# One encoder layer on one core: convolution tiles made four ahead, query tiles transposed inside the last output product, first weight loaded in parts

## The reference, cut to what matters

```python
def token_mixer(x, ...):             # x: 1024 prompt rows and 8 x 16 sample rows of 1024
    proj = x @ w_in                  # query and latent parts, gates gb, gc, gv
    ...                              # attention of 8 heads (prompt: chunk-causal; sample: 512 cached rows too)
    u = gc * gv
    conv = cw[0]*u[s-2] + cw[1]*u[s-1] + cw[2]*u[s]
    return concat(attn, gb * conv) @ w_out
mk, mv = mem @ w_xk, mem @ w_xv      # 256 memory rows
x1 = LN1(alpha*x + token_mixer(x))
x2 = LN2(alpha*x1 + softmax((x1 @ w_xq) mk^T * scale) mv @ w_xo)
x3 = LN3(alpha*x2 + moe(x2))         # 32 gated experts, two per row
```

## Time and profile before

| what | us |
|---|---|
| median of 3 runs (1803.07 to 1812.1) | 1804.54 |
| the profiled execution, its own time | 1816.85 |
| its span, first to last instruction | 1815.0 |
| TensorE busy | 1653.2 (91% of the span) |
| VectorE busy | 1011.5 (56%) |
| ScalarE busy | 756.0 (42%) |
| GpSimd busy | 236.3 (13%) |

### The profile page before, as it was taken

How to read it: one execution, slowest core, us unless ns; L and a number is a source line. 1 busy time by engine, 2 the same in 40 slices (tenths; PEclk the granted TensorE clock), 3 DMA queues, 4 the chain that set the end, 5 groups by cost and what they waited for, 6 DMA issues and landing times.

```text
span 1815.0 us, 21425 instructions
## 1 busy us (share of the span) xinstructions
PE 1653.2 (91%) x8118; PEld 1280.6 (71%) x8118; DVE 1011.5 (56%) x1365; ACT 756.0 (42%) x1077; POOL 236.3 (13%) x192
## 2 busy tenths in 40 slices
PE   6999999799998797999989999699999999999965
PEld 3466666477667575899977777678888888888852
DVE  0301111166664375512244444698889889988946
ACT  0211221233335200222241212188777778788844
POOL 0000000000003165000011110111111111111104
PEclk9899999999999899999999987699999999999998
DMA  9401111420001443410034444489999999999967
GB/s 383 144 9 64 62 56 44 163 77 18 19 12 47 162 140 116 149 49 24 12 116 151 148 143 151 169 326 378 367 369 385 382 393 382 383 385 384 370 249 301
DMA packets 134692, 348.59 MB, mean 192 GB/s; under 512 B 24514, under 2 KB 27074, under 8 KB 129364
## 3 DMA queue, kind: packets, MB, share of 16 engines
q1 hardware_dynamic: 125396, 328.60, 49.2%
q0 software_dynamic: 9216, 18.89, 2.7%
HBM read 320.09 MB, written 42.10 MB: 200 GB/s over the span
## 4 chain that ended last, share of the span: by engine, by line
PE 60%; DMA 17%; DVE 13%; ACT 4%; issue 3%; SPq 2%; POOL 1%; DVEq 0%; POOLq 0%; ACTq 0%
DMA beside<-in_w_exp_up 13%; PE M L1118 9%; DVE rounded L1568 8%; PE M L683 8%; PE M L877 8%; PE T L723 6%; PE M L782 3%; PE T L674 3%; PE T L772 3%; PE M L674 2%; PE T L929 2%; PE T L930 2%; PE T L931 2%; PE M L956 2%; PE M L943 2%
## 5 line engine op out<-in xcount | busy, mean ns | idle before, releaser
L1118 PE MATMUL M<-rounded 128*128 128x512 f32 x2304 | 548.9, 395 | 13.4 <-DVE conv_w_rows L1883 7.7
L1118 PEld LDWEIGHTS M<-rounded 128*128 128x128 f32 x2304 | 430.0, 189 | 106.8 <-issue 16.0
L1568 DVE TENSOR_TENSOR rounded<-beside,rounded 128x1024 fp32r<-128x1024 f32 x395 | 462.8, 1217 | 63.1 <-ACT rounded L1454 55.3
L1454 ACT CAST rounded<-beside 128x1024 fp32r<-128x1024 f32 x256 | 260.3, 1049 | 96.1 <-DMA beside<-in_w_exp_up 83.3
L877 PE MATMUL M<-rounded 128*128 128x512 f32 x864 | 224.8, 418 | 9.9 <-issue 7.5
L877 PEld LDWEIGHTS M<-rounded 128*128 128x128 f32 x864 | 171.4, 202 | 50.7 <-issue 14.4
L683 PE MATMUL M<-arena 128*128 128x512 f32 (+1 forms) x352 | 145.4, 574 | 10.2 <-DMA arena<-in_w_xk 6.8
L1464 ACT CAST rounded<-beside 128x1024 fp32r<-128x1024 f32 x128 | 126.2, 1048 | 20.0 <-DMA beside<-in_w_exp_down 14.7
L683 PEld LDWEIGHTS M<-arena 128*128 128x128 f32 x352 | 68.3, 195 | 83.8 <-issue 72.1
L674 PE MATMUL T<-tables,arena 128*128 128x128 f32 x564 | 79.7, 291 | 45.0 <-POOL arena L2078 17.7
L674 PEld LDWEIGHTS T<-tables,arena 128*128 128x128 f32 x564 | 69.0, 150 | 61.5 <-POOL arena L2078 19.8
(11 more groups left out here) (286 smaller groups left out, 1999.9 us busy)
## 6 DMA issues: line engine op xcount, KB each, us to landing
beside<-in_w_exp_gate SPq DMA_DIRECT2D x64, 1024.0 KB, 8.3
beside<-in_w_exp_up SPq DMA_DIRECT2D x64, 1024.0 KB, 11.2
beside<-in_w_exp_down SPq DMA_DIRECT2D x32, 2048.0 KB, 11.7
arena<-x_rows SPq DMA_DIRECT2D x27, 512.0 KB, 3.6
x_rows<-arena SPq DMA_DIRECT2D x18, 512.0 KB, 4.4
arena<-expert_rows SPq DMA_DIRECT2D x9, 1024.0 KB, 12.6
arena<-in_x_prompt SPq DMA_DIRECT2D x16, 512.0 KB, 4.5
arena<-in_cache_mem_k SPq DMA_DIRECT2D x8, 1024.0 KB, 5.7
```

The costliest lines, as they stand in the source:

```text
L1118: got = nc.tensor.matmul(out, x[xs], (high, low)[ws](w)[:, c:c + 512], start=(first and n == 0), stop=(last and n == 2))
L1454: nc.scalar.copy(high(c), w_raw[c // 4][:, c % 4, :]).then_inc(gu_high, 1)
L1568: return nc.vector.tensor_tensor(out, x, highs.bitcast(f32), ALU.subtract)
```

## The change

Four things change. (1) Only the identity is loaded ahead of the memory rows, and the other tables behind w_xv. w_xk comes in four transfers of 1 MB, and its product runs over k outermost, for both row tiles at once, with a wait for a quarter before every second k. Both tiles are then reported together. (2) The convolution is made four tiles ahead, with four result buffers: tiles 0 to 3 during the sample attention, tile t+4 behind the deviation of tile t. The 25 transfers of the sample's tile are issued by ScalarE, after it rounded tile 5 and the convolution of tile 6 is done. Three working buffers of the sample attention lie elsewhere, so that both convolution buffers are free in it. (3) VectorE waits for gain and shift just ahead of the first norm. (4) In the sample's output product TensorE transposes the first two query tiles, tile 1 after step 1 and tile 0 after step 3. ScalarE and VectorE take tile 1 after chunk 2 of w_xq and tile 0 after chunk 6 (ScalarE when the whole product is done). The split rows lie one tile after the other, so each matmul of the queries reads 2 x 128 columns, 2048 elements apart, in place of 256 in a row. The first eighth of the queries waits for w_xq chunk by chunk.

```diff
@@ memory
-        latTb, krTb, p_b = pair(WORK, PAST), pair(WORK + 1056, PAST), pair(WORK + 2112, PAST + ROWS)
+        latTb, krTb, p_b = pair(KEEP + 1024, PAST), pair(41216, PAST), [area(at, PAST + ROWS) for at in (WA + 17472, 42240)]
...
-        x1T_hi, x1T_lo = (rounded[:, 20480 + half * 2048:22528 + half * 2048].rearrange("p (k c) -> p k c", k=KT) for half in (0, 1))
+        x1T = rounded[:, 20480:24576].rearrange("p (u s k c) -> p s k u c", u=2, s=2, k=KT)
...
-        conv_rows = pair(46848, CW)
+        conv_rows = [area(at, CW) for at in (46848, 47360, 45312, 45824)]
@@ SyncE, opening
-            sp.dma_start(tables, A["tables"]).then_inc(mem_in, 16)
+            sp.dma_start(ident, A["tables"][:, 0:P]).then_inc(mem_in, 16)
             sp.dma_start(mem, mem_rows).then_inc(mem_in, 16)
-            sp.dma_start(w_xk, by_rows("w_xk")).then_inc(wxk_in, 16)
+            for q in range(4):
+                sp.dma_start(w_xk[:, 2 * q:2 * q + 2, :], by_rows("w_xk")[:, 2 * q:2 * q + 2, :]).then_inc(ring_in[q], 16)
             sp.dma_start(w_xv, by_rows("w_xv")).then_inc(wxv_in, 16)
+            sp.dma_start(tables[:, P:], A["tables"][:, P:]).then_inc(consts_in, 16)
@@ SyncE, convolution
             def load_conv(t):
-                w = 0 if t == 0 or t % 2 == 1 else 1
+                w = (t + 1) % 2
                 cv = (cv0, cv1)[w]
-                if t > 0:
-                    sp.wait_ge(conv_ready, 1 if t < 3 else t - 1)
-                if t == PT:
-                    for k in range(3):
-                        for b in range(NB):
-                            sp.dma_start(cv[b * ROWS:(b + 1) * ROWS, k, :], us_dram[b, k:k + ROWS, :]).then_inc(conv_in[w], 16)
-                else:
-                    for k in range(3):
-                        sp.dma_start(cv[:, k, :], u_dram[t * P + k:(t + 1) * P + k, :]).then_inc(conv_in[w], 16)
+                if t > 1:
+                    sp.wait_ge(conv_ready, t - 1)
+                for k in range(3):
+                    sp.dma_start(cv[:, k, :], u_dram[t * P + k:(t + 1) * P + k, :]).then_inc(conv_in[w], 16)
                 sp.dma_start(cv[:, 3, :], gb_dram[t * P:(t + 1) * P, :]).then_inc(conv_in[w], 16)
...
-            load_conv(0)
-            load_conv(1)
+            for t in range(4):
+                load_conv(t)
...
-            load_conv(2)
             load_x(1)
...
-            load_conv(3)
             for t in range(PT - 1):
+                if t + 4 < PT:
+                    load_conv(t + 4)
                 store_x1(t)
-                if t + 4 <= PT:
-                    load_conv(t + 4)
                 load_x(t + 2)
@@ TensorE
-            pe.wait_ge(wxk_in, 16)
-            for c in (0, 1):
-                pe.wait_ge(mem_act, c + 1)
-                product(M[c], memT[:, c, :, :], w_xk, BOTH).then_inc(mem_ps, 1)
+            pe.wait_ge(mem_act, 2)
+            for k in range(KT):
+                if k % 2 == 0:
+                    pe.wait_ge(ring_in[k // 2], 16)
+                for c in (0, 1):
+                    for c0, c1 in BOTH:
+                        got = nc.tensor.matmul(M[c][:, c0:c1], memT[:, c, k, :], w_xk[:, k, c0:c1], start=(k == 0), stop=(k == KT - 1))
+            got.then_inc(mem_ps, 2)
...
-                transposes(T[u][:, 512:], conv_rows[u], 4).then_inc(rowsT_ps, 1)
+                transposes(T[u][:, 512:], conv_rows[t % 4], 4).then_inc(rowsT_ps, 1)
...
                     if t == PT:
                         got.then_inc(w_used, 1)
+                        if k in (1, 3):
+                            turn_x1(1 - k // 2, xa[0][1 - k // 2])
...
-                            nc.tensor.matmul(out, high(k)[:, d * P:(d + 1) * P], x1T_hi[:, k, :], start=(k == 0), stop=False)
...
+                            if j == 0 and d == 0:
+                                pe.wait_ge(w_low, 2 * KT + k + 1)
+                            nc.tensor.matmul(out, high(k)[:, d * P:(d + 1) * P], x1T[:, 0, k], start=(k == 0), stop=False)
...
-            turn_x1(0, xa[0][0])
-            turn_x1(1, xa[0][1])
-            pe.wait_ge(w_low, 3 * KT)
@@ ScalarE (VectorE has the same two calls in its own loop over the low parts)
+                if t == 5:
+                    act.wait_ge(conv_ready, PT - 1)
+                    for b in range(NB):
+                        for k in range(3):
+                            nc.scalar.dma_start(cv1[b * ROWS:(b + 1) * ROWS, k, :], us_dram[b, k:k + ROWS, :]).then_inc(conv_in[1], 16)
+                    nc.scalar.dma_start(cv1[:, 3, :], gb_dram[PT * P:, :]).then_inc(conv_in[1], 16)
...
                 nc.scalar.copy(high(k), raw).then_inc(w_high, 1)
+                if k == 2:
+                    turn_x1(1, 0)
+                if k == 6:
+                    act.wait_ge(w_used, KT)
+                    turn_x1(0, 1)
...
-            act.wait_ge(w_used, KT)
-            turn_x1(0)
-            turn_x1(1)
@@ VectorE
-            dve.wait_ge(ln_in, 32)
...
                 mix_low(t + 1)
+                if t == 1:
+                    dve.wait_ge(ln_in, 32)
                 if t > 0:
                     norm_rows(t - 1, (t - 1) % 2, xr, res, gain1, shift1).then_inc(norm_ready, 1)
@@ GpSimd
             def convolve(t):
...
-                if t > 1:
-                    pool.wait_ge(rowsT_ps, t - 1)
-                out = conv_rows[t % 2]
+                if t > 3:
+                    pool.wait_ge(rowsT_ps, t - 3)
+                out = conv_rows[t % 4]
...
-            convolve(0)
-            convolve(1)
+            for t in range(4):
+                convolve(t)
             for t in range(PT):
-                if t + 2 < NT:
-                    convolve(t + 2)
                 deviation(t, t % 2)
+                if t + 4 < NT:
+                    convolve(t + 4)
```

More of the change, by code:

```diff
@@ L234, in encoder_layer_kernel @@
         ring += [beside[:, at - ROUNDED:at - ROUNDED + D] for at in (41216, 42240)]
-        wq_raw = [(ring[k % 6], *((0, 96) if k < 6 else (k - 5, 16))) for k in range(KT)]
-        wo_raw = [(ring[k % 4], *((3, 64) if k < 4 else (k - 4, (112, 32, 32, 80)[k - 4]))) for k in range(KT)]
+        wq_raw = [(ring[k % 6], *((0, 112) if k < 6 else (k - 5, 32))) for k in range(KT)]
+        wo_raw = [(ring[k % 4], *((3, 80) if k < 4 else (k - 4, (128, 48, 48, 96)[k - 4]))) for k in range(KT)]
         rows_hi, rows_lo = ([rounded[:, 20480 + u * 2048 + half * D:20480 + u * 2048 + half * D + D] for u in (0, 1)] for half in (0, 1))
-        x1T_hi, x1T_lo = (rounded[:, 20480 + half * 2048:22528 + half * 2048].rearrange("p (k c) -> p k c", k=KT) for half in (0, 1))
+        x1T = rounded[:, 20480:24576].rearrange("p (u s k c) -> p s k u c", u=2, s=2, k=KT)
         gain1, shift1 = area(KEEP, D), area(KEEP + D, D)
@@ L893, in turn_mix, with turn_x1 @@
                     transposes(T[u], attn[:, t, :], 4)
-                transposes(T[u][:, 512:], conv_rows[u], 4).then_inc(rowsT_ps, 1)
+                transposes(T[u][:, 512:], conv_rows[t % 4], 4).then_inc(rowsT_ps, 1)
+            def turn_x1(t, rows):
+                u = t % 2
+                pe.wait_ge(x_in[u], 16 * (2 * (5 - u) + t // 2 + 1))
+                transposes(T[u], rows, KT).then_inc(rowsT_ps, 1)
             turn_mix(0)
@@ L910, in _ @@
                         got.then_inc(w_used, 1)
+                        if k in (1, 3):
+                            turn_x1(1 - k // 2, xa[0][1 - k // 2])
                 if t < PT:
                     got.then_inc(product_ps, 1)
-            def turn_x1(t, rows):
-                u = t % 2
-                pe.wait_ge(x_in[u], 16 * (2 * (5 - u) + t // 2 + 1))
-                transposes(T[u], rows, KT).then_inc(rowsT_ps, 1)
             def queries(j):
@@ L928, in queries @@
                         for k in range(KT):
-                            nc.tensor.matmul(out, high(k)[:, d * P:(d + 1) * P], x1T_hi[:, k, :], start=(k == 0), stop=False)
-                            nc.tensor.matmul(out, high(k)[:, d * P:(d + 1) * P], x1T_lo[:, k, :], start=False, stop=False)
-                            got = nc.tensor.matmul(out, low(k)[:, d * P:(d + 1) * P], x1T_hi[:, k, :], start=False, stop=(k == KT - 1))
+                            if j == 0 and d == 0:
+                                pe.wait_ge(w_low, 2 * KT + k + 1)
+                            nc.tensor.matmul(out, high(k)[:, d * P:(d + 1) * P], x1T[:, 0, k], start=(k == 0), stop=False)
+                            nc.tensor.matmul(out, high(k)[:, d * P:(d + 1) * P], x1T[:, 1, k], start=False, stop=False)
+                            got = nc.tensor.matmul(out, low(k)[:, d * P:(d + 1) * P], x1T[:, 0, k], start=False, stop=(k == KT - 1))
                     got.then_inc(qT_ps, 1)
@@ L981, in _ @@
                     pe.wait_ge(rows_low, NT + NT)
-                    hi, lo = ([x[:, k, 0:P] for k in range(KT)] for x in (x1T_hi, x1T_lo))
+                    hi, lo = ([x1T[:, s, k, 0, :] for k in range(KT)] for s in (0, 1))
```

(16 more changed lines are left out.)

31 lines of the change are left out of this document (13 added, 18 removed).

## The result

The changed kernel takes 1792.94 us (median of 7 runs, 1787.74 to 1797.35) where the kernel before took 1807.46 on the same chip (7 runs, 1803.07 to 1815.26): a ratio of 0.9914, 95% interval 0.9886 to 0.9942. That is 15.5 us gained, 10.5 to 20.6, about half of the 29.2 forecast, and 1792.94 lies above the range. Of the 17.6 us between it and the forecast 1775.3, 2.9 are the kernel before, which took 1804.54 in the runs that the forecast started from and 1807.46 here; 14.7 are gain that didn't come, by the two medians. The profiled execution took 1796.74 us, its span 1794.9, so between the two profiles 20.1 us went.

A forecast was written before the change was run, and what follows sets the result against it. The chain was held by w_xk's load in the opening and TensorE's 17.7 us of convolution waits in the output product. Opening -6.9, sample attention +1.3 and output product to queries -23.6 gave -29.2 us: 1775 us, range 1765 to 1786.

The forecast's parts named there:

- Opening, -6.9: Opening: w_xk's product starts at 11.1 and ends at 40.3, not 47.30; -6.9 us, bounds -5.2 to -8.6.
- that rival: Opening: w_xk's quarters land out of order, or the gates' loads bound it, so the part does nothing; 1782, 8%.
- Sample attention, +1.3: Sample attention: two more convolutions beside it give VectorE's chain two short hits; +1.3 us, between 0 and +7.
- the upper bound of 7: Sample attention: a whole 3.5 us GpSimd multiplication is waited for twice; up to 7 us in place of 1.3.
- Start, -4.9 and -2.9: Output product's start: begins at 614.4, not 619.28 (-4.9 us); first tile warm, 11.13 not 13.98 (-2.9 us).
- Tiles 0 to 8: Output product: no convolution late for TensorE; last product starts at 709.6, where before it was about 736.2.
- The wait of 1.1 for a low part: Output product: TensorE waits once, 1.1 us, for VectorE's low part of tile 7.
- Dear issues on ScalarE: Output product: ScalarE's 25 transfer issues cost 1.0 us each, not 0.48, delaying tile 6's rounding; 1783, 15%.
- Query tiles in the last product: Last output product: moved transposes (1.9 us) wait 5.2 us for input, cooling the clock for about 1.8; queries from 730.1.
- Clock at the queries, -2.2: Start of the queries: the first 24 matmuls no longer run cold; -2.2 us.
- the slower rival: Queries: the moving operand in two pieces reads at the cold rate, 71 us more; 1846, 3%.
- Full blocks (1781): Sample attention: each added convolution stops one chain instruction for its whole multiplication, +7 for +1.3; 1781, 7%.

The follow-up runs named there:

- the pair of repeats: Kernel before and changed kernel, both unchanged, timed and profiled again on another chip: 1807.77 us (0.9981) and 1787.15 us (0.9889).
- the opening alone: Kernel before with only the change's opening (tables after w_xv, w_xk in four parts, product step by step for both row tiles): 1802.36 us, 0.9962.
- the kernel with the split: Changed kernel with GpSimd's convolution multiplication of 128x1536 made as three of 128x512: 1786.18 us, 0.9870.
- the gap: Changed kernel with convolutions 2 and 3 late and reads early, plus GpSimd waiting for the second batch's scaled probabilities before convolution 1: 1775.42 us, 0.9823.
- early reads: Changed kernel with the two normalized tiles read back ahead of tile 6's store and the sample's residual rows: 1782.76 us, 0.9871.
- late and early: Changed kernel with convolutions 2 and 3 after the sample attention and the two tile reads early: 1780.25 us (0.9834), again 1778.18 us (0.9840).

## Why the prediction was wrong, by its own steps

**Opening, -6.9: right, and a little small.** It measured -7.9 in the change and -8.1 alone. The 1 us more is the end that the bounds named as the warm one: 27.73 for 29.22. In the two executions with a product of 29.33 and 29.93 it was -6.3 and -5.8, also inside the bounds of -5.2 to -8.6. No quarter was late, so that rival is out.

**Sample attention, +1.3: this step failed**, and it alone carries 8.3 of the 9.1 us by which the two profiles miss the sum. In the pair of repeats it misses by 6.2 (+7.5 for +1.3). Two things were wrong in it.

The first is the size of a block. The step took the one row of this very instruction beside a convolution, 1.27 for 0.49, as its price. That was a grazing hit: the scaling came at 575.50, 2.6 us into a multiplication of 3.56 us (572.93 to 576.49). The cost has no fixed size; it is what is left of the GpSimd instruction when VectorE asks. Asked just after a 3.4 us multiplication began, 0.49 becomes 3.13, as the norm had already shown with 4.03 for 0.80. The Trainium skill, page "SBUF — State Buffer", section "SBUF: two separate sides", says that whichever of such a VectorE operation and a GpSimd operation starts first holds the shared ports for its whole length. By that rule, the trace agrees: 577.19 to 580.62 on GpSimd, 577.78 to 580.91 on VectorE, and thirds of the multiplication brought the longest to 1.33. I had both and took the milder row; the upper bound of 7 was the better value. Nor did the step count the low parts, which stand in the same queue and took 3.1 us more in all.

The second is the clock, for which the forecast had no term here. The matmuls at L827 to L830 of a cold batch take 4.61 us (0.58 + 0.43 + 1.89 + 1.71), those of the one at 573 take 2.40 (0.37 + 0.22 + 0.95 + 0.86), and the transposes behind them double too. That is 2.2 us for the matmuls of each cold batch, and two batches were cold.

The runs divide the 9.6, in part. From 53.41 to 56.12, 2.7, comes with the opening alone, where the clock falls from 561 to 572: not the work of the added convolutions, and not of the part of the change that touches this stage. Against the repeat of the kernel before it is only 0.9. From 56.12 to 57.17, 1.1, comes with the rest of the change but no added convolution: 0 and 1 now follow one another, and the eight scalings take 6.0 for 5.2. From 57.17 to 63.01, 5.8, comes with convolutions 2 and 3: their blocks, and the second cold stretch, which went when they were held back and also when their multiplications were split with all of GpSimd's work in place. These are differences of single executions: the versions with a repeat moved by 0.2, 1.8 and 3.4 us, the last two by their clock. So the 2.7 and the 1.1 aren't shown one by one, and the 5.8 is too high as a size: the four executions with convolutions 2 and 3 whole took 60.5 to 63.0, 62.0 in the mean, and the six with them held back 57.1 to 61.2, 58.2 in the mean. That the added convolutions cost something like 4 us is shown; the ranges touch, through an execution that was cold before the first convolution ended.

**Start, -4.9 and -2.9: right.** 3.54 us from transposes to product against 8.20, and the first tile at 11.15: -4.7 and -2.8. (As written, 613.0, 1.0 and 1.2 add up to 615.2; the 614.4 counts from the end of the first tile's eight transposes, about 1 us earlier.) The second term was the clock of one execution: in the repeat of the kernel before that tile took 12.65, and the same step would be worth 1.5.

**Tiles 0 to 8: right.** No wait for a convolution. The wait of 1.1 for a low part didn't come; 0.53 stands there, put down to issue. Dear issues on ScalarE are out: 0.49 each, 11.86 for 24. (The row that the forecast read its 0.48 from, 12.07 for 24, gives 0.50.)

**Query tiles in the last product: right in mechanism and size.** The reads were issued at 712.47, the wait measured 5.62 (forecast 5.2), and the stall's cold clock 2.0 (forecast 1.8). The 2.0 is luck in part: in the repeat, behind 6.08, the same 12 matmuls lost 0.5, and in the kernel with the split, behind 2.43, 1.6 (4.58). From transposes to queries 121.23 came of 120.8 forecast. But the step read its own sum too kindly: it booked -23.2 for start, tiles and turn together and never asked what the moved transposes brought by themselves. In this stretch they cost 6.1 to 7.7 against leaving them behind the product.

**Clock at the queries, -2.2: missed, and not the change's to give.** The queries' first matmuls still ran cold (spacing 0.21 from 734.5 to 737.7), after an idle time of only 2.41. In the repeats both kernels ran them warm, 0.12 from the start: the 24 cold matmuls of the earlier trace rows were a matter of the one execution. The split moving operand costs nothing, 0.12 where the clock is up, so the slower rival is out. (The 1.94 for 16 transposes that the forecast gave to the memory rows is the output product's; the memory rows' took 3.42. The comparison stands.)

**Full blocks (1781)** was the rival with the right mechanism, at 7% far too cheap. Its +7 stands against +9.6 and, in the repeats, +7.5; it too lacked the clock. With the measured 9.6 in place of the 1.3 the sum is -20.9, where the profiles have -20.1. Why the runs gave 15.5 is not shown; the spread of the last stretch would be enough, and the same kernel gave 0.9914 and 0.9889, whose intervals both hold 20.

**The runs beat both kernels.** With two convolutions held back and the reads issued early, the time is 1780.25 and 1778.18, and 1775.42 with the gap: by the medians some 27 to 34 us less than the kernel before. That the gap adds to it isn't shown.

## What to carry to other kernels

An instruction of GpSimd like this one, beside a dependent chain of VectorE, costs what is left of it when VectorE asks. So price it at its full length once per convolution, and count every VectorE instruction in that queue that a row shows stretched (here the scaling and the low part, not the maximum out of PSUM). Splitting it made the longest block shorter, 1.33 for 3.13; try that before you move it there, and time it. Work moved forward needs its input forward too: ask of the queue that feeds it what stands ahead, and time the moved part against leaving it where it was. Where a chain is stretched in a stage in which TensorE works in short turns, put in a term for its clock. A clock read from one execution is worth a second one before it enters a sum.

## What the runs showed of the hardware that I had not expected

The granted clock fell in the sample attention although no single wait of TensorE there was over 2.9 us (six waits for VectorE, 7.7 us together), while elsewhere it stayed at 1.00 over an idle 2.94; and after the same idle time of 2.41 ahead of the queries it read, in two executions of different versions:

```profile
725.10:729.00 3.90, 3.88 (x21) 3.90 (x22) 3.83 (x4) 0.00 (x0) 0.00 (x0) 0.59 0.00 0
```

```profile
719.10:723.00 3.90, 3.87 (x32) 3.90 (x33) 3.83 (x4) 0.00 (x0) 0.00 (x0) 1.00 0.00 0
```

(first early reads, then late and early). The changed kernel did both itself: 733.50 to 737.40 at 0.61, and in its repeat 731.90 to 735.80 at 1.00, each behind 2.41. The length of the wait alone doesn't say which of its two levels (1.2 and 2.4 GHz) the clock takes. What does was not tried.

Left open as well: why the opening alone, whose part of the program ends some 470 us earlier, brought a cold stretch into the sample attention. TensorE's timeline of the stage is the same up to it. From the first matmul to the end of the wait in which the clock falls it takes 13.20 us (549.94 to 563.14), in the kernel before 13.19 (557.67 to 570.86), and that wait is 1.40 and 1.39. Then the clock reads 0.50 from 564 to 568 in the one and 1.00 from 572 to 576 in the other. One execution can't tell this from chance, and nothing was run for it.
